# A two-block layer on one core: the first routing query summed during the output projection, with another order of tile 1's values and of the gather slots

## The reference

```
x = x + gt1 * (merged @ w_out)
h2 = modulate(rms_norm(x, g_ffn), sh2, sc2)          # h * (1 + scale) + shift
q = (h2 @ w_pq).reshape(T, 8, 2, 128)
sub = einsum('thpc,hpnc->thpn', q, peer_keys)
s_top, i_top = top_k(sub, 16); best_s, pos = top_k(pair sums, 16); gate = softmax(best_s)
act = gelu(einsum('cd,ckd->ck', x_c, peer_u[expert]))
out = einsum('ck,ckd->cd', gate * act, peer_v[expert])
```

## Time and profile before

| what | us |
|---|---|
| median of 3 runs | 1400.97 (1399.03 to 1401.54) |
| profiled execution | 1398.66 |
| its span on the profile | 1396.9 |
| TensorE busy in it | 1271.5 (91%) |
| VectorE busy | 777.0 (56%) |
| ScalarE busy | 329.3 (24%) |
| GpSimd busy | 296.8 (21%) |

### The profile page before, as it was taken

One profiled execution on the slowest core, in us unless ns is written; L12 is line 12 of the kernel. 1 busy time (PEld: TensorE's weight loads), 2 busy tenths in 40 slices (PEclk: granted clock), 3 DMA queues, 4 the chain that ended last, 5 costly groups with the idle time before them and its releaser, 6 DMA issues.

```text
span 1396.9 us, 14350 instructions
## 1 busy us (share of the span) xinstructions
PE 1271.5 (91%) x4688; PEld 715.0 (51%) x4688; DVE 777.0 (56%) x2107; ACT 329.3 (24%) x858; POOL 296.8 (21%) x271
## 2 busy tenths in 40 slices
PE   6899999999999987879899999898987899999998
PEld 4688975566555553434444444434332344544444
DVE  6256556786866775787747575764656542220002
ACT  2412133432211231232212212111100043311102
POOL 0000014343433342343122332232323000000000
PEclk9999999999999998989999999999999999999999
DMA  9999979999999999999999999999999998688882
GB/s 370 405 346 350 383 266 401 384 419 417 417 417 417 417 390 419 378 366 418 416 416 415 411 408 417 409 416 401 417 416 416 392 413 306 210 259 288 288 303 92
DMA packets 107256, 519.87 MB, mean 372 GB/s; under 512 B 12208, under 2 KB 12976, under 8 KB 73904
## 3 DMA queue, kind: packets, MB, share of 16 engines
q0 software_dynamic: 41088, 285.23, 50.3%
q1 hardware_dynamic: 63648, 228.22, 43.4%
q10 hardware_dynamic: 2448, 5.51, 1.2%
HBM read 516.29 MB, written 1.05 MB: 370 GB/s over the span
## 4 chain that ended last, share of the span: by engine, by line
PE 65%; DMA 26%; DVE 5%; ACT 2%; issue 2%; SPq 0%; POOL 0%; DVEq 0%; ACTq 0%; POOLq 0%
PE ps_M L941 27%; DMA ring<-in_w_second 11%; PE ps_T L753 9%; PE ps_T L754 8%; DMA arena<-in_peer_uv,arena 5%; DMA ring<-in_w_pq 5%; PE ps_M L663 4%; DMA ring<-in_peer_uv,arena 4%; PE ps_M L494 3%; PE ps_M L722 2%; PE ps_M L517 1%; PE ps_M L686 1%; DMA ring<-in_w_in 1%; PE ps_M L506 1%; PE ps_SA L722 1%
## 5 line engine op out<-in xcount | busy, mean ns | idle before, releaser
L941 PE MATMUL ps_M<-ring,arena 128*128 128x512 f32 x1072 | 492.7, 600 | 38.8 <-DMA ring<-in_w_second 38.3
L941 PEld LDWEIGHTS ps_M<-ring,arena 128*128 128x128 f32 x1072 | 195.6, 191 | 279.2 <-issue 220.2
L1248 POOL DMA_INDIRECT ring<-in_peer_uv,arena x137 | 154.1, 1125 | 332.7 <-PE ps_T L754 302.4
L1248 POOL DMA_INDIRECT arena<-in_peer_uv,arena x105 | 120.4, 1146 | 249.8 <-PE ps_T L754 232.6
L753 PE MATMUL ps_T<-ring,arena 128*128 128x512 f32 x230 | 125.4, 628 | 24.7 <-ACT arena L1387 24.6
L1376 ACT ACTIVATE arena<-arena 128x2 f32<-128x2 f32 x128 | 25.8, 202 | 416.9 <-DVE arena L2086 410.3
L754 PE MATMUL ps_T<-ring,arena 128*128 128x512 f32 x230 | 120.9, 608 | 0.0
L2066 DVE SCALAR_TENSOR_TENSOR ring<-ring,merged 128x1024 f32<-128x1024 f32 x72 | 87.7, 1221 | 43.2 <-DMA ring<-in_peer_uv,arena 43.2
L753 PE MATMUL ps_T<-arena 128*128 128x512 f32 x178 | 94.9, 615 | 16.8 <-ACT arena L1387 16.7
L2066 DVE SCALAR_TENSOR_TENSOR ring<-ring,arena 128x1024 f32<-128x1024 f32 x65 | 79.3, 1221 | 31.4 <-DMA ring<-in_peer_uv,arena 30.8
L754 PE MATMUL ps_T<-arena 128*128 128x512 f32 x178 | 93.1, 605 | 0.0
(11 more groups left out here) (310 smaller groups left out, 1488.5 us busy)
## 6 DMA issues: line engine op xcount, KB each, us to landing
ring<-in_w_second SPq DMA_DIRECT2D x274, 512.0 KB, 9.2
ring<-in_w_in SPq DMA_DIRECT2D x66, 512.0 KB, 10.2
arena<-in_w_ada POOLq DMA_DIRECT2D x8, 2048.0 KB, 14.3
ring<-in_w_pq SPq DMA_DIRECT2D x28, 512.0 KB, 9.5
arena<-in_w_ada SPq DMA_DIRECT2D x16, 512.0 KB, 15.1
ring<-in_w_out SPq DMA_DIRECT2D x16, 512.0 KB, 5.8
ring<-in_w_br SPq DMA_DIRECT2D x16, 384.0 KB, 7.9
ring<-in_peer_uv,arena POOLq DMA_INDIRECT x137, 11.6
```

Of the source, the lines that this page charges most:

```text
L941: m = mm(bank, left[c], w[:, c, :], start=first and c == 0, stop=last and c == 1)
L1248: pool.indirect_dma_start(row_slots[s], None, A["peer_uv"], bass.IndirectOffsetOnAxis(ap=expert[:, u % 3, k:k + 1], axis=0))\
```

## The change

It computes the same output. The first query of tile 0 is no longer multiplied from normed and shifted features: VectorE multiplies each block of x by the gain as soon as the output projection has produced it (`first_gain`), the shift stands as a 129th column beside the 128 tokens (`gained`), and TensorE adds a block at a time to banks T0 and T1 (`first_query`), ten matmuls behind the sixth block of the output projection, two behind the seventh, four behind the eighth. ScalarE copies the query out and spreads the 129th column to 128 (`shift_spread`); TensorE multiplies both by the keys (now banks OT and S1); ScalarE copies the shift's scores (`shift_scores`), and VectorE multiplies the query's scores by the token's norm factor and adds them (`first_take`). The factor as a column comes from the diagonal of the norm sum (`first_factor`).

The normed and shifted features, which the rows, the other queries and the gates need, are made behind the first `route_index`. The two value products come ahead of `turn_rows` and query 1 on TensorE, and on ScalarE `stick_soft1(0)` comes ahead of query 1's copies and of `score_take(1)`. The slots are taken in another order, and slot 3 (`tmp`), which now still holds the squares, is waited for.

```diff
-CYCLES = (3, 4, 6, 2, 0, 1, 5, 7, 8), (6, 2, 0, 1, 5, 7, 8)
+CYCLES = (4, 6, 0, 1, 3, 7, 8, 2, 5), (6, 0, 1, 7, 8, 2, 5)
...
+            def first_query(half, c):
+                w = tile(("q0", half))
+                pe.wait_ge(gain_ready, c + 1)
+                m = mm(ps[f"T{half}"][:, 0:P + 1], w[:, c, :], gained[:, c, :], start=c == 0, stop=c == KC - 1)
+                if c == KC - 1:
+                    finish(m, ("q0", half))
...
-                bank = claim(("OT", "T0")[half], name)
+                bank = claim(("OT", "S1")[half], name)
                 pe.wait_ge(*emptied(("q0", half)))
+                mm(bank[:, NK:2 * NK], shift_cols[:, half, :], keysT[:, half, :], start=True, stop=True)
...
+                for c in {5: range(5), 6: (5,), 7: (6,)}.get(k, ()):
+                    for half in range(2):
+                        first_query(half, c)
+            first_query(0, KC - 1)
             norm_part(KC - 1)
-            stick_scores1(0)
+            first_query(1, KC - 1)
             pe.wait_ge(key_in, 16)
             for half in range(2):
-                query(0, half)
                 half_scores(half)
+            stick_scores1(0)
+            values(("ldvA", 1), 1, [("ldv", j) for j in range(4)])
+            values(("lsv", 1), 1, [("lsv", j) for j in range(SB_PAIRS)])
             for half in range(2):
                 turn_rows(0, half, f"T{half}")
             for half in range(2):
                 query(1, half)
             scores(1)
-
-            values(("ldvA", 1), 1, [("ldv", j) for j in range(4)])
             for name in late_gates(-1)[0:2]:
                 tile_gate(1, name)
-            values(("lsv", 1), 1, [("lsv", j) for j in range(SB_PAIRS)])
...
+                if s == OWN and held is None:
+                    pool.wait_ge(h_norm2, KC // 2)
+                    pool.wait_ge(h_high, KC // 2)
+                elif held is not None:
...
+            act.wait_ge(*produced(("q0", 0)))
+            F(qT[:, 0, :], ps["T0"][:, 0:P], ACT.Copy).then_inc(st.tick(), 1)
+            shift_spread(0)
+            act.wait_ge(*produced(("q0", 1)))
+            F(qT[:, 1, :], ps["T1"][:, 0:P], ACT.Copy).then_inc(st.tick(), 1)
+            act.wait_ge(first_sum, 1)
+            F(first_root[:, 1:2], first_root[:, 0:1], ACT.Sqrt, bias=eps, scale=1.0 / D).then_inc(first_sqrt, 1)
+            shift_scores(0)
+            shift_spread(1)
+            shift_scores(1)
             tile_root(("norm2", 0), 0)
+            stick_old(0)
             tile_shift(0)
-            for half in range(2):
-                query_take(0, half)
-                copy(("sub", 0, half), sub[:, 0, half, :], NK)
+            copy(("ldvA", 1), vd[:, 1, 0:512], 512)
+            gate_expo(0)
+            copy(("lsv", 1), vs[:, 1, :], SBW)
             for half in range(2):
                 copy(("rows", 0, half), h_rows[0][:, half * 512:(half + 1) * 512], 512)
-            stick_old(0)
+            stick_soft1(0)
             for half in range(2):
                 query_take(1, half)
-            gate_expo(0)
             score_take(1)
-            stick_soft1(0)
-            copy(("ldvA", 1), vd[:, 1, 0:512], 512)
...
+            def first_factor():
+                dve.wait_ge(*produced(("norm2", 0)))
+                V.scalar_tensor_tensor(hot.rearrange("p a b -> p (a b)")[:, 0:P], ps["SA"][:, 0:P], 1.0, ident[:, :], ALU.mult, ALU.mult,
+                                       accum_out=first_root[:, 0:1]).then_inc(first_sum, 1)
+                dve.wait_ge(first_sqrt, 1)
+                V.reciprocal(first_root[:, 2:3], first_root[:, 1:2]).then_inc(st.tick(), 1)
+            def first_take(half):
+                dve.wait_ge(*produced(name))
+                dve.wait_ge(shift_scored, half + 1)
+                V.scalar_tensor_tensor(sub[:, 0, half, :], bank[:, 0:NK], first_root[:, 2:3], sub[:, 0, half, :], ALU.mult, ALU.add)
...
             for k in range(KC):
                 out1_update(0, k)
+                first_gain(k)
+            first_factor()
+            for half in range(2):
+                first_take(half)
+                route_half(0, half)
+            candidates()
+            top8(best[:, 0, :], pos, cand.rearrange("p a b -> p (a b)"))
+            route_index(0, 0, 8)
             tile_scale(0)
...
-            route_half(0, 0)
-            route_half(0, 1)
-            candidates()
-            top8(best[:, 0, :], pos, cand.rearrange("p a b -> p (a b)"))
-            route_index(0, 0, 8)
             next8(best[:, 0, :], pos, cand.rearrange("p a b -> p (a b)"), cand_w)
```

More of the change, by code:

```diff
@@ L289, in build @@
         own_rows = carve(OWN, 2 * D)
+        gained = arena[:, carved[0]:carved[0] + KC * (P + 1)].rearrange("p (c t) -> p c t", t=P + 1)
         h_rows0 = carve(D)
@@ L394, in build @@
         merged_tile, x_out1 = sem("merged_tile"), sem("x_out1")
+        gain_ready, first_sum, first_sqrt, shift_scored = (
+            sem(n) for n in ("gain_ready", "first_sum", "first_sqrt", "shift_scored"))
         idx_ready, best_ready, gate_exp = sem("idx_ready"), sem("best_ready"), sem("gate_exp")
@@ L719, in query @@
                 for c in range(KC):
-                    if u in (0, NH) and half == 0:
+                    if u in (1, NH) and half == 0:
                         pe.wait_ge(*row_block_there(t, c))
@@ L1485, in beside @@
                 at = (phase, k)
-                if at == (-1, 4):
-                    copy(("lsv", 1), vs[:, 1, :], SBW)
-                elif at == (-1, 6):
+                if at == (-1, 6):
                     stick_prob1(0)
@@ L1970, in tile_inverse, with first_gain @@
                 own()
+            def first_gain(c):
+                V.tensor_scalar(gained[:, c, 0:P], xT[:, c, tile_tok(0)], gain2[:, c:c + 1], None, ALU.mult).then_inc(gain_ready, 1)
+            def first_factor():
+                dve.wait_ge(*produced(("norm2", 0)))
+                dve.wait_ge(ident_in, 16)
+                V.scalar_tensor_tensor(hot.rearrange("p a b -> p (a b)")[:, 0:P], ps["SA"][:, 0:P], 1.0, ident[:, :], ALU.mult, ALU.mult,
+                                       accum_out=first_root[:, 0:1]).then_inc(first_sum, 1)
+                dve.wait_ge(first_sqrt, 1)
+                V.reciprocal(first_root[:, 2:3], first_root[:, 1:2]).then_inc(st.tick(), 1)
+                own()
+            def first_take(half):
+                name = ("sub", 0, half)
+                bank = ps[use[name][0]]
+                dve.wait_ge(*produced(name))
+                dve.wait_ge(shift_scored, half + 1)
+                V.scalar_tensor_tensor(sub[:, 0, half, :], bank[:, 0:NK], first_root[:, 2:3], sub[:, 0, half, :], ALU.mult, ALU.add)\
+                    .then_inc(released(name), 1)
             def tile_scale(t):
@@ L2155, in _ @@
             own()
+            V.tensor_scalar(gained[:, :, P], mod[3], 1.0, None, ALU.mult).then_inc(st.tick(), 1)
+            own()
             for k in range(KC):
                 out1_update(0, k)
+                first_gain(k)
+            first_factor()
+            for half in range(2):
+                first_take(half)
[3 more added lines that the diff above has]
+            route_index(0, 0, 8)
             tile_scale(0)
@@ L2160, in _ @@
             for c in range(KC // 2, KC):
[L2161 to L2168 removed]
+                V.tensor_scalar(hT[:, c, tile_tok(0)], squares[:, c, :], mod[3][:, c:c + 1], None, ALU.add).then_inc(h_high, 1)
             next8(best[:, 0, :], pos, cand.rearrange("p a b -> p (a b)"), cand_w)
```

17 lines of the change are left out of this document (12 added, 5 removed).

## The result

The changed kernel takes 1401.74 us (median of 20 runs, 1398.57 to 1404.17), the kernel before 1399.38 us beside it (20 runs): ratio 1.0018, 95% interval 1.0011 to 1.0025. It is 2.5 us slower (1.5 to 3.5). The forecast was +4.4 us on 1400.97, the median of three runs, so 1405.4 us. The time lies in the range; the direction is right, the size is not. Of the 3.7 us by which 1405.4 is too high, 1.6 come from the base (three runs at 1400.97, twenty at 1399.38) and 2.1 from the forecast of the change.

A forecast was written before the change was run, and what follows sets the result against it. Neither TensorE nor DMA alone was taken as the bound; TensorE's use of row 11 times later gathers. 3.7 us there plus 0.7 for the clock gave +4.4 on 1400.97, so 1405.4 us, range 1397.5 to 1409.

The forecast's parts named there:

- carried rigidly from row 11 to the end: From row 11's use to the kernel's end: the summed delay of 4.4 us passes through whole.
- the clock term: Stick scores and first value product: a longer low clock after idling at 188 to 193 us adds 0.7 us (0 to 1.7).
- First gather 3.4 us earlier, worth nothing: Start of gathering: first gather at 199.0 us, 3.4 us earlier; the DMA time won is used up before 240 us.
- The rival that the start of gathering decides: Start of gathering: DMA times row 11, so the 3.4 us come through, 1397.6 or 1395.3 us; chance 0.15.
- First accumulation 2.3 us late: TensorE's first accumulation: at 223.05 us against 220.73, behind the softplus, query 1's copies, route of unit 1 and dots.
- Row 11 and with it gather 20 3.7 us late: Behind the first accumulation: VectorE loses its lead, reaches the stick-sum subtraction 3.7 us late, and row 11 is used as late.
- The DMA gap forecast at 266 us: DMA windows near gather 20: a sign of being right, gaps at 266 us as before or larger.
- The rival "absorbed": New ScalarE and VectorE chain 1 to 2 us shorter, queue slack takes some: only 0 to 2.3 us left, 1402; chance 0.22.
- Slots, nothing: Row slots during gathering: each later gather still takes the slot of nine, then seven, rows before, so the distance stays.
- The late weights at the end: End of gathering: weight tiles behind row 255 come late, TensorE stops, up to 3 us more, 1408; chance 0.05.

The follow-up runs named there:

- e6: Changed kernel with its row slots back in the order of the kernel before, so the first gather goes back by 3.7 us; 1401.26 us, ratio 1.0017.
- e12: Kernel before with four of tile 1's lsv matmuls done twice, as a pure delay; 1403.57 us, ratio 1.0027.
- e1: Changed kernel with ScalarE's first stick softplus back behind the copies of query 1 and of unit 1's scores; 1402.45 us, ratio 1.0018.
- e2: e1 plus tile 1's lsv values behind unit 1's scores on TensorE, their copy behind the softplus, and e3's slot order; 1397.27 us, ratio 0.9992.
- e9: Changed kernel measured again, nothing edited; 1401.99 us, ratio 1.0019 to the kernel before.
- e3: Changed kernel with only the slot order edited, so the ring slots are given back at rows 249 to 252; 1402.40 us, ratio 1.0020.
- e7: Changed kernel with e1's ScalarE order, e3's slots, lsv behind the gate tiles on TensorE and its ScalarE copy in the row loop; 1398.60 us, ratio 1.0006.
- e10: e2 with the two gate tiles moved into the row loop, on TensorE behind the first accumulation; 1394.47 us, ratio 0.9975 to the kernel before.
- e8: Kernel before with only the changed kernel's slot order; 1402.35 us, ratio 1.0020.
- e4: Kernel before with ScalarE's first stick softplus ahead of query 1's copies, as a pure delay; 1410.04 us, ratio 1.0077.
- e5: Kernel before with tile 1's values ahead of the row transposition and query 1 on TensorE, and the changed kernel's ScalarE order; 1404.69 us, ratio 1.0045.
- e14: Kernel before with seven of tile 1's lsv matmuls done twice, as a pure delay; 1407.46 us, ratio 1.0049.
- e13: Kernel before with two of tile 1's lsv matmuls done twice, as a pure delay; 1400.07 us, ratio 1.0006.

## Why the prediction was right and wrong

The step that failed is the last of the sum, "carried rigidly from row 11 to the end", and ahead of it the clock term was put in the wrong place. The sum has 4.4 us at row 20 and at the end; measured are 3.9 at row 20 and 2.5 (1.5 to 3.5) in the times.

- **First gather 3.4 us earlier, worth nothing.** Right: 3.45, and e6, which takes it away, loses nothing. The rival that the start of gathering decides falls. The rows show two idle stretches ahead of the slow query, 0.62 and 0.81 us, and not three; e12 prices that fall at 1.1 us.
- **First accumulation 2.3 us late.** Right: 2.13, by the chain that was named: softplus, query 1's copies, scores, route of unit 1, dot. The waits were forecast at 2.4 and 4.2 us and are 1.96 and 4.05. Of the two causes given, ScalarE's order counts for 1.8 us there and for 0.8 at gather 20 (e1), the place of the values for most of the rest (e2). (The terms behind VectorE's route add up to 222.95 and not 223.05 us, a slip of 0.1.)
- **Row 11 and with it gather 20 3.7 us late.** The mechanism is right, the size in part by luck: 3.9. VectorE's lead is gone (4.35 us of waiting became 0.71). Its own chain accounts for 3.2 us; the other 0.7 are its wait for matmuls slowed by the clock. The DMA gap forecast at 266 us "as before or larger" is smaller: a share of 0.85 at 268 to 270 us, for 0.78 at 262 to 264 before. The large gap came at 226 to 230 us.
- **The clock, +0.7.** Wrong in its place, and near in size by luck. No fall met the stick scores or the first value product; the granted clock was 1.00 from 186 to 197 us. The fall came where the forecast had left it out, behind the wait of 4.05 us: 0.50 at 226 to 228 us, the lower of the two levels (1.2 GHz) throughout, with accumulations of 1.66 and 1.92 us for 1.02. e9 shows the same mean, 0.72 over 224 to 230 us. The Trainium skill, "TensorE: Matmul & The Clock Gate", section "HAM oscillation — how this bites in real kernels", names idle gaps between bursts as the cause. The trace agrees that the clock fell behind such a gap. Of the 1.7 us that I had priced a whole fall at (3.60 for 1.87 us), 0.7 reached the chain. L576 ended late and VectorE, which timed the stage, waited 0.71 us for it. At 0.86 us from one group of two pieces to the next, as from 230 us on, L576 would have ended at 228.7, 1.1 us before VectorE needed it (an estimate from these rows). e9, e3 and e6 show the same wait, 0.70 or 0.71; in e1 it is 1.64; in e7 the fall met the value product, 8.65 us for 7.03. In e10, whose wait is 0.76 us, the clock stayed at 1.00.
- **Carried rigidly to the end.** This is where the sum fails: 3.9 at row 20 are 2.4 to 2.8 in the times. From gather 20 to 460 us it holds to 0.2 us in every trace but e3's (0.5) and e8's, because the DMA engines are full. In e4, e5, e12 and e14 the times carry the whole delay (10.8 for 11.0, 6.3 for 5.0, 3.8 for 3.5, 6.9 for 6.1), in e13 half of it (0.8 for 1.8); the four kernels that start 3.9 us late and contain the changed first query (changed, e9, e3, e6) lie at 2.4 to 2.8, with spans of 1.9 to 3.3. Where they give back some 1.3 us stays open: behind 460 us the scatter of the traces covers it (there two traces of one kernel differ by 1.7 at 700 us, and e14's grew by 4). Of the four intervals only that of the 20 runs ends below 3.9, at 3.5. All 56 runs of the four together, each against the runs of before beside it, give 2.7 us (2.0 to 3.5, by resampling the medians), so the times do lose less than 3.9. The marks begin at the output projection, whose start scatters from 168.5 to 173.2 us over the 16 traces of this case (8 of either first query, 3 late starts in each), and no run shows where the 1.2 us went. The rival "absorbed" has the measured time (1402) but not the way to it: its condition was a shorter chain and slack in the queue, and gather 20 is 3.9 us late.
- **Slots, nothing.** Right for this kernel, for a reason that was not general (e8). The late weights at the end cost nothing that shows (2.8 us without them in e3, 2.5 with them).
- **That the change does what it says.** It does: half 0's top 8 at 22.1 us behind the start, where it was 24.8.

## What to carry to other kernels

Before a step is brought forward, ask which work stands in the waits behind it: here the value products, `lsv` above all, were the filling between TensorE's last result and the first diagonal, and 3.45 us won at the head turned into 3.9 lost at row 20 when they were moved. What mended it was work put back into the wait, piece by piece and with its PSUM bank in the account (e7 failed on a bank, e10 won 3.5 us on the kernel before). A wait also slowed what stood behind it: the fall of the clock cost 0.7 us of the 3.9, and 1.6 in e1, by way of another engine that waited for the slowed matmuls. And the gain at the head of the stream counted for nothing here, because the engine that empties the slots did not come earlier too.

## What the runs showed that I had not expected

- The clock ahead of the change differs from execution to execution and moves every later mark. In ten of the 16 traces the granted clock is 0.91 over 60 to 80 us and the output projection starts at 168.5 to 169.1 us, in six it is 0.83 and the start lies at 170.4 to 173.2; kernels with and without the change are in both groups. Marks have to be taken from a point that both kernels share.
- With every row's slot the same and gather 20 at the same place to 0.1 us, the DMA engines had moved 2.6 us less in e8. Bytes moved tell more than one gather's time.
- e14's delay of 6.1 us grew to 10.3 between 560 and 700 us in its trace, while its times say 6.9: behind row 60 one trace is worth about 2 to 4 us of uncertainty, however exact it is ahead of it.
